# A two-layer encoder step on one core: weight blocks moved by 16 bytes, rows of the MLP's inner tiles at another pitch

## What is computed

```
def sq_relu_mlp(x, g, w_up, w_down):
    return jnp.square(jax.nn.relu(rmsnorm(x, g) @ w_up)) @ w_down

for layer in range(DEPTH):                      # DEPTH = 2, D_MODEL = 2048
    ...                                         # u = rmsnorm(h, g_mix); h = h + mix(u @ w_in) @ w_out
    hp = hp + sq_relu_mlp(hp, norm_mlp[layer], mlp_w_up[layer], mlp_w_down[layer])
    hs = hs + sq_relu_mlp(hs, norm_mlp[layer], mlp_w_up[layer], mlp_w_down[layer])
```

## Time and profile before

| what | value |
|---|---|
| runs shown | 2862.0, 2862.4, 2863.89 us; median 2862.4 |
| the profiled execution | 2863.7 us |
| its span, first to last instruction | 2861.7 us |
| mean granted TensorE clock | 0.999 |
| TensorE busy | 2843.7 us, 18,666 matmuls |
| VectorE, ScalarE, GpSimd busy | 1428.0, 1069.6, 186.0 us |
| read from HBM | 396.48 MB, 141 GB/s over the span |

### The profile page before, as it was taken

The page is one execution under the profiler, slowest core; times in us unless marked ns, Lnnn a source line. Parts: engine busy times, 40 slices in busy tenths (PEclk is TensorE's granted clock), DMA queues, the critical chain, the costliest instruction groups (busy, mean ns, idle before and its releaser), DMA issues.

```text
span 2861.7 us, 45023 instructions
## 1 busy us (share of the span) xinstructions
PE 2843.7 (99%) x18666; PEld 2798.6 (98%) x18666; DVE 1428.0 (50%) x1546; ACT 1069.6 (37%) x1236; POOL 186.0 (7%) x112
## 2 busy tenths in 40 slices
PE   9999999999999999999999999999999999999999
PEld 9997799999999999999999999899999999999999
DVE  7677645543443344344466774546444443444443
ACT  5334533332332333233335633434333332432332
POOL 2000002000000000000221241112000000000000
PEclk9999999999999999999999999999999999999999
DMA  6433024444444444444444444244444444444443
GB/s 232 139 114 111 30 89 143 144 140 145 143 140 148 140 145 142 141 146 140 145 149 155 154 146 148 97 160 149 148 152 151 148 152 149 148 152 149 149 153 135
DMA packets 112783, 405.25 MB, mean 142 GB/s; under 512 B 12656, under 2 KB 14752, under 8 KB 112480
## 3 DMA queue, kind: packets, MB, share of 16 engines
q1 hardware_dynamic: 108864, 392.64, 41.2%
q0 software_dynamic: 1616, 6.31, 0.6%
q10 hardware_dynamic: 2128, 3.66, 0.3%
HBM read 396.48 MB, written 6.09 MB: 141 GB/s over the span
## 4 chain that ended last, share of the span: by engine, by line
PE 97%; DVE 2%; ACT 1%; issue 0%; DMA 0%; ACTq 0%; DVEq 0%
PE PS L1426 31%; PE PS L1430 30%; PE PS L1431 30%; PE PS L1505 0%; ACT pr L498 0%; DVE pr L925 0%; DVE w_lo L858 0%; PE PS L1706 0%; DVE rb L1067 0%; PE PS L1503 0%; PE PS L1881 0%; PE PS L1489 0%; ACT w_hi L450 0%; PE PS L1753 0%; PE PS L1752 0%
## 5 line engine op out<-in xcount | busy, mean ns | idle before, releaser
L858 DVE TENSOR_TENSOR w_lo<-stage,w_hi 128x1024 fp32r<-128x1024 f32 x734 | 919.6, 1255 | 1192.6 <-ACT w_hi L450 1192.2
L450 ACT ACTIVATE w_hi<-stage 128x1024 fp32r<-128x1024 f32 x740 | 784.0, 1060 | 1628.2 <-PE PS L1431 1618.7
L1426 PE MATMUL PS<-xh,w_hi 128*128 128x336 f32 (+1 forms) x3264 | 1021.5, 313 | 1.1 <-DVE kk L1102 0.6
L1430 PE MATMUL PS<-xl,w_hi 128*128 128x336 f32 (+1 forms) x3248 | 1015.3, 313 | 0.0
L1431 PE MATMUL PS<-xh,w_lo 128*128 128x336 f32 (+1 forms) x3248 | 1014.6, 312 | 0.0
L1426 PE MATMUL PS<-hh,w_hi 128*128 128x336 f32 (+1 forms) x2032 | 635.2, 313 | 0.0
L1431 PE MATMUL PS<-hh,w_lo 128*128 128x336 f32 (+1 forms) x2032 | 635.1, 313 | 0.0
L1430 PE MATMUL PS<-hl,w_hi 128*128 128x336 f32 (+1 forms) x2032 | 634.9, 312 | 0.0
L1426 PEld LDWEIGHTS PS<-xh,w_hi 128*128 128x128 f32 x3264 | 614.4, 188 | 3.9 <-DVE w_hi L848 1.1
L1431 PEld LDWEIGHTS PS<-xh,w_lo 128*128 128x128 f32 x3248 | 612.1, 188 | 0.0
L1430 PEld LDWEIGHTS PS<-xl,w_hi 128*128 128x128 f32 x3248 | 611.5, 188 | 0.4
(11 more groups left out here) (343 smaller groups left out, 1527.7 us busy)
## 6 DMA issues: line engine op xcount, KB each, us to landing
stage<-in_wstream SPq DMA_DIRECT2D x740, 512.0 KB, 3.3
out_s<-so POOLq DMA_DIRECT2D x8, 256.0 KB, 2.6
x<-in_x_in SPq DMA_DIRECT2D x6, 336.0 KB, 7.2
out_y<-x ACTq DMA_DIRECT2D x3, 672.0 KB, 4.0
dmask<-in_ret POOLq DMA_DIRECT2D x4, 352.0 KB, 6.1
stage<-in_wstream SPq DMA_DIRECT2D x4, 256.0 KB, 3.6
s<-in_s_in POOLq DMA_DIRECT2D x1, 1024.0 KB, 5.3
x<-in_x_in SPq DMA_DIRECT2D x4, 168.0 KB, 3.7
```

Of the source, the lines that this page charges most:

```text
L450: act.activation(w_hi[s], halves_of(s), ACT.Copy).then_inc(hi_ready, 1)
L858: dve.tensor_tensor(w_lo[s], halves_of(s), w_hi[s].bitcast(F32), ALU.subtract).then_inc(lo_ready, 1)
L1426: pe.matmul(out, wh, rh, start=first, stop=False)
L1430: pe.matmul(out, wh, rl, start=False, stop=False)
```

## The change

The tiles w_hi and w_lo keep their size and place, but each block of weights begins four numbers (16 bytes) further on in its row; ScalarE's and VectorE's writes and TensorE's reads go through the same slices and move with it. The tiles hh and hl become flat tiles of 16 x 340 + 64 numbers, with a view of 16 rows for each layer: a first number and a step. In layer 0 hh has step 336 from number 0, and hl step 337 from number 56; in layer 1 both have step 337 from number 32. Steps of 336 and 337 numbers are 1344 and 1348 bytes. Everything else in the diff picks the layer's view. Instructions, their order, their sizes and all waits stay as they are.

```
         def split_blocks(name):
             flat = keep(name, [P, NR * UNIT + WPAD], F32R)
-            return [flat[:, WAT[s]:WAT[s] + 2 * WROW].rearrange("p (j c) -> p j c", j=2)[:, :, 0:512]
+            return [flat[:, WAT[s]:WAT[s] + 2 * WROW].rearrange("p (j c) -> p j c", j=2)[:, :, 4:516]
                     for s in range(NR)]
...
-        HB = TB + 16
-        hh = place("hh", [P, 16, T + 4], B, F32R)
-        hl = place("hl", [P, 16, T + 4], B + 16 * HB, F32R)
-        mt1 = place("mt1", [P, 4, T], B + 32 * HB)
-        mt2 = place("mt2", [P, 4, T], B + 32 * HB + 4 * TB)
+        HROWS = 16 * (T + 4) + 64
+        hh_all = place("hh_all", [P, HROWS], B, F32R)
+        hl_all = place("hl_all", [P, HROWS], B + 4 * HROWS, F32R)
+
+        def h_rows(tile, first, step):
+            return tile[:, first:first + 16 * step].rearrange("p (k t) -> p k t", t=step)
+
+        hh = [h_rows(hh_all, 0, T), h_rows(hh_all, 32, T + 1)]
+        hl = [h_rows(hl_all, 56, T + 1), h_rows(hl_all, 32, T + 1)]
+        mt1 = place("mt1", [P, 4, T], B + 8 * HROWS)
+        mt2 = place("mt2", [P, 4, T], B + 8 * HROWS + 4 * TB)
...
-                dve.tensor_tensor(hl[:, 4 * c:4 * c + 4, cs], mt2[:, :, cs], hh[:, 4 * c:4 * c + 4, cs].bitcast(F32),
+                dve.tensor_tensor(hl[L][:, 4 * c:4 * c + 4, cs], mt2[:, :, cs], hh[L][:, 4 * c:4 * c + 4, cs].bitcast(F32),
                                   ALU.subtract).then_inc(hl_ready, 1)
...
-                        chunk(u_mlp + 32 + CU * c, g_mlp + 4 + c, hh, hl, f, 64, 8, cs=COLS[n],
+                        chunk(u_mlp + 32 + CU * c, g_mlp + 4 + c, hh[L], hl[L], f, 64, 8, cs=COLS[n],
```

More of the change, by code:

```diff
@@ L532, in body @@
                         act.wait_ge(hsq_done, at(f, 4, g + 1))
-                        act.activation(hh[:, 4 * c:4 * c + 4, cs], mt2[:, :, cs], ACT.Copy).then_inc(hh_ready, 1)
+                        act.activation(hh[L][:, 4 * c:4 * c + 4, cs], mt2[:, :, cs], ACT.Copy).then_inc(hh_ready, 1)
                     for c in range(4):
@@ L1930, in _ @@
             for c in range(3):
-                chunk(u0 + 32 + CU * c, g0 + 4 + c, hh, hl, cs=LIVE,
+                chunk(u0 + 32 + CU * c, g0 + 4 + c, hh[1], hl[1], cs=LIVE,
                       need=(lambda k: pe.wait_ge(hl_ready, 16 + 12 + k // 2 + 1)) if c == 0 else None)
-            chunk(N_UNITS - CU, G_END - 1, hh, hl, cs=LIVE, ks=range(CU - 2))
+            chunk(N_UNITS - CU, G_END - 1, hh[1], hl[1], cs=LIVE, ks=range(CU - 2))
             pe.wait_ge(lo_ready, N_UNITS)
@@ L1939, in _ @@
                     out = PS[:, 4 * ((G_END - 1) % 2) + o, LIVE]
-                    pe.matmul(out, wh, hh[:, kt, LIVE], start=False, stop=False)
-                    pe.matmul(out, wh, hl[:, kt, LIVE], start=False, stop=False)
-                    mm = pe.matmul(out, wl, hh[:, kt, LIVE], start=False, stop=kt == KT - 1)
+                    pe.matmul(out, wh, hh[1][:, kt, LIVE], start=False, stop=False)
+                    pe.matmul(out, wh, hl[1][:, kt, LIVE], start=False, stop=False)
+                    mm = pe.matmul(out, wl, hh[1][:, kt, LIVE], start=False, stop=kt == KT - 1)
                 mm.then_inc(y_done, 1)
```

## The result

The changed kernel takes 2869.26 us (median), the kernel before 2862.82 us in the same measurement: a ratio of 1.0023, 95% interval 1.0014 to 1.0031. It is slower, where I had forecast 2851 us and faster. The profiled execution is 2868.84 us long, its span 2866.8 us. The medians lie 6.4 us apart, with an interval of 4 to 9 us; what follows divides up the 5.1 us between the spans of the two profiled executions.

What follows compares the result with a forecast made beforehand. TensorE's matmul pace was taken as the bound. Half of the distance to the best rows, (10.7 + 2.2 + 6.3 + 2.7)/2 = 11.0 us, came off, giving 2851 us, 0.4% faster, range 2836 to 2870 us.

Steps and rivals of the forecast that it cites:

- What bounds the kernel: Whole kernel: TensorE, busy 2843.7 of 2861.7 us; matmul count is unchanged, so only its pace can change the time.
- Part (3): ScalarE and VectorE writing off the grid: even a tenth longer stays hidden behind TensorE; costed at nothing.
- Part (1): Matmuls on w_hi or w_lo, blocks 16 bytes on: 10.7 + 2.2 us saved at best rows' pace, half taken; 15.1 us lost at 336.
- row 15: Fastest hh k-row at 336 columns, 48 bytes off the grid: 1.82 us, taken as the pace moved blocks could give xh.
- Part (2): Matmuls on re-spaced hh and hl rows: 2.1 us saved at xh's pace, 9.0 at the best row's; half of 9.0 taken.
- The grid of 64: Places against 64 bytes: streams and blocks all on one grid meet most regularly; only rows off it run faster.
- Rows 7: xh matmuls after a gate unit in layer 1's input projection: 154.32 ns instead of 153.48 on the grid, read as history.
- The third one: Rival: hh and hl rows straddling 16-byte lines cost 1.8 ns each, 5.5 us, giving 2867.9; chance 0.07.
- The first rival: No change: 16 bytes leave the common rhythm, only the hh and hl part remains, 2860 to 2866 us; chance 0.34.

Runs made afterwards that it cites:

- e12: Kernel before with hh and hl rows 1408 bytes apart on multiples of 64, where e3 has 1344: 2865.01 us.
- e14: e3 with hh and hl moved on together by 128 bytes: 2867.48 us.
- e6: e3 with the weight blocks 16 bytes further on: 2861.27 us, ratio 0.9993 to the kernel before.
- e3: Kernel before with all rows of hh and hl 1344 bytes apart on multiples of 64, like xh; blocks as before: ratio 0.9993.
- e9: The same kernel as e3, timed again with more runs: ratio 0.9990 to the kernel before.
- e2: Changed kernel with the weight blocks back in their old place, so only hh and hl moved: 2863.8 us, ratio 1.0002 to the kernel before.
- e15: e3 with hh and hl moved on together by 192 bytes: 2861.7 us.
- e8: e3 with low rows moved off their high rows: xl 16 bytes on, hh 64, hl 96: 2873.87 us.
- e1: Kernel before with only the weight blocks 16 bytes further on, hh and hl as before: 2865.85 us, ratio 1.0009.
- e4: Kernel before with every row of hh and hl starting 4 bytes later, pitch 1360 bytes as before: 2881.48 us, ratio 1.0063.
- e5: Kernel before with the weight blocks 4 bytes further on, hh and hl as before: 2880.41 us.
- e13: e3 with hh and hl moved on together by 64 bytes: 2865.12 us.

## Why the prediction was wrong

**What bounds the kernel: right.** All of the result is TensorE's pace; the count of matmuls, TensorE's waits and the times of the other engines' operations are as before, and the list of stretches adds up to 5.0 of the 5.1 us by which the span grew.

**Part (3), the writing engines: right.** 1255 and 1059 ns where 1255 and 1060 stood; their cover is untouched.

**Part (1), the blocks: wrong in sign.** The step that failed is the value taken, half of the distance to the best row, -6.4 us. It rested on reading the 1.82 us of row 15 as the price of its place, 48 bytes on. With the blocks moved, every xh row has just that place, and takes 153.47 ns in the MLP at 336 columns, as before. e12 beside e14 shows why the inference was not allowed: distance 192 takes 155.9 ns in a row between other rows and 154.3 in a stretch of its own. Nor is the pace one for all: the gate units change the distance, and behind the third of them the changed kernel has the faster pace that the prediction hoped for, 152.9 ns instead of 154.3, but for 192 matmuls only. What the term really measured is 0 in the MLP at 336 columns and -0.27 us behind that gate unit; at 320 columns +1.3 us in xh (only where the hh products hand on the slower pace, e6), +0.4 us in moh and +0.22 us behind the first gate unit. The recorded upper end of this term is a little off too: 155.8 - 153.48 is 2.3 ns, 14.6 us, not 2.4 and 15.1. Nothing rests on it.

**Part (2), hh and hl: wrong in sign as well.** Taken at half of 9.0 us saved; measured 4 x 0.25 + 4 x 0.57 = 3.3 us lost. The smaller bound that stood beside it, that hh would take the pace of the xh rows for 2.1 us, is what e3 and e9 deliver; but it needs rows like those of xh, and the change has hl in layer 0, and both in layer 1, 1348 bytes apart. Alone (e2) this part is worth 0.4 us, -1.2 in layer 0 and +1.6 in layer 1.

**The grid of 64: wrong.** The prediction took "off the grid" for the way out of a slow rhythm. e12 to e15 show that the grid is not what counts. The distance of row and block modulo 256 bytes counts, though it is not all: the rows before decide too (e6). Of the four distances on the grid, those which the kernel before has in its xh products, 64 at 336 columns and 128 at 320, are the fastest at 336 and among the fastest at 320. That something off the grid is faster is not refuted: 152.9 ns at distance 176 behind the gate unit and e8's 144.7 at 320 columns are. No run has the MLP at either.

**Rows 7: misread.** I took two paces at one alignment for history; e14 gives the same pace by distance. That history matters is true nevertheless, but it is e6 against e1 that shows it, at 320 columns.

**The rivals.** The third one has a likely cause with too small a size: 1.8 ns for a straddled line, where e4 measured 2.5 and 2.9 when all rows straddle. The Trainium skill, in "SBUF — State Buffer", section "Specifications (TRN2)", has 16-byte lines with a penalty for each crossing; e4 and e5 agree, but change the distance as well. By rows that straddle alone the change would have cost nothing at 336 columns and 1.6 us at 320 (e2), and the time of 2867.9 that it gave is near the result for a good part by chance. That the two parts make each other worse (118.32 and 113.24 against e2's 117.78 and 113.06, while e1 leaves hh at 118.06 and 112.72) stood nowhere. The first rival, no change, is what e1 and e2 are singly. I gave faster 0.46 on the ground that the only fast rows were off the grid, but of the sixteen rows one was faster than the xh products and six were slower; the even reading of that was no change, or a small loss.

## What to carry to other kernels

When TensorE streams four-byte operands back to back, its pace depends on where token rows and weight blocks lie relative to each other. If the pitches of both differ by a multiple of 256 bytes (here 2112 - 1344 = 3 x 256), the distance modulo 256 stays the same from step to step, and one number sets the layout. That number has to be tried: a constant distance of 64 gave 117.87 us at 336 columns, one of 128 gave 118.70, more than the 118.07 of the mixed rows before. Start all rows on 16-byte boundaries (e4). Measure such a layout by stretches of one product in the trace, which resolve about 0.01 ns a matmul where the whole program resolves 0.1%. A time of one row inside a varied pattern is not the price of its address, and one part's gain alone (e2 in layer 0) does not survive a second part that moves the other operand.

## What was not expected of the hardware

- The pace has a value that many layouts reach to the digit, 153.47 ns for 336 columns and 146.25 for 320 (e3, e6, and xh in the MLP of nearly all runs), and at 320 columns, where all k-rows are alike, losses come in steps of 6.67 ns a k-row, the time of 16 columns at the granted 2.4 GHz. It is no floor: 29.36/192 = 152.9 behind the third gate unit of the changed kernel, 27.79/192 = 144.7 in e8. Against the columns alone these are still 13 and 11 ns a matmul; no layout tried here took that away.
- Stream and weight load are not independent. The Trainium skill, "TensorE: Matmul & The Clock Gate", Part 2 ("What happens when you issue a matmul"), gives TensorE two independent read ports for them. From that one would expect the place of one against the other to be free; here moving the token rows by 64 bytes against the blocks changes 117.87 us into 118.70 (e13) with nothing else touched. Where stream and load meet is not shown.
- With the same addresses, a product can run at two paces for hundreds of microseconds, 112.32 or 112.75 us a stretch, by what ran before it (e6, e1), and behind two small matmuls and a pause of 0.24 us it was at the faster one again (changed kernel). How this state is carried over the stretches is open.
- Why 320 columns react to a block 4 bytes on with 2.7 ns and 336 columns with 0.5 (e5), and which of the 13 ns is whose, is open too.
